# Latent items of a two-layer diffusion step: one multiplication per head, copies and squares ahead of the gate, three items' transposes behind the first scores

## The reference, cut to what matters

```python
aq, ak, av, bq_d, bkv_d, cq, ck, cv, gates = jnp.split(h @ p['w_in'], IN_SPLITS, axis=-1)
bq = (rms_norm(bq_d, p['mla_q_norm']) @ p['w_mla_q_up']).reshape(b, t, MLA_HEADS, MLA_QK_DIM)
bq = rms_norm(bq, p['mla_qk_norm'][0])
...
kv = (rms_norm(ckv, p['mla_kv_norm']) @ p['w_mla_kv_up']).reshape(b, s, MLA_HEADS, MLA_NOPE_DIM + MLA_V_DIM)
k = rms_norm(jnp.concatenate([k_nope, k_pe], axis=-1), p['mla_qk_norm'][1])
...
ck = rms_norm(ck.reshape(b, t, GQA_KV_HEADS, HEAD_DIM), p['gqa_qk_norm'][1])
```

## Time and profile before

| | us |
|---|---|
| median of 3 runs | 2578.64 (2576.64 to 2580.96) |
| the profiled execution | 2574.08 |
| its span | 2571.3 |
| PE busy in the span | 2485.4 (97%) |
| DVE busy | 1368.3 (53%) |
| ACT busy | 972.0 (38%) |
| POOL busy | 410.2 (16%) |
| mean granted clock of PE | 0.986 |

### The profile page before, as it was taken

One profiled execution on the slowest core, in us unless ns is written; L12 is line 12 of the kernel. 1 busy time (PEld: TensorE's weight loads), 2 busy tenths in 40 slices (PEclk: granted clock), 3 DMA queues, 4 the chain that ended last, 5 costly groups with the idle time before them and its releaser, 6 DMA issues.

```text
span 2571.3 us, 42771 instructions
## 1 busy us (share of the span) xinstructions
PE 2485.4 (97%) x17115; PEld 2262.6 (88%) x17115; DVE 1368.3 (53%) x2339; ACT 972.0 (38%) x1713; POOL 410.2 (16%) x362
## 2 busy tenths in 40 slices
PE   7999999999999999999999999999999999999998
PEld 5878977798799999999977799768978999999998
DVE  4675366736755454254446734765476545433542
ACT  5453255424534332133244523454254243322332
POOL 0500022022020221022014001220310202200220
PEclk8999999999999999999999999999999999999999
DMA  7312232422132222322322021322210412222222
GB/s 241 96 34 66 70 102 79 130 88 59 34 115 66 66 81 62 86 66 70 122 79 74 18 79 60 96 88 66 79 49 17 145 52 69 74 74 78 81 58 82
DMA packets 252834, 202.80 MB, mean 79 GB/s; under 512 B 9877, under 2 KB 235911, under 8 KB 252679
## 3 DMA queue, kind: packets, MB, share of 16 engines
q1 hardware_dynamic: 245574, 197.67, 25.5%
q10 hardware_dynamic: 7104, 2.95, 0.4%
HBM read 196.50 MB, written 4.10 MB: 78 GB/s over the span
## 4 chain that ended last, share of the span: by engine, by line
PE 89%; DVE 4%; ACT 4%; issue 1%; DMA 1%; SPq 1%; POOL 0%; ACTq 0%; POOLq 0%; DVEq 0%
PE ps L1376 48%; PE ps L1398 8%; PE ps L1549 6%; PE ps L1563 4%; PE ps L1590 4%; PE ps L1361 3%; PE ps L1363 3%; PE ps L1362 3%; PE ps L1488 1%; PE ps L1445 1%; PE ps L1251 1%; ACT prob L1834 1%; PE ps L1505 1%; PE ps L1508 1%; PE ps L1261 1%
## 5 line engine op out<-in xcount | busy, mean ns | idle before, releaser
L2056 DVE TENSOR_TENSOR wlo<-raw,whi 128x1024 fp32r<-128x1024 f32 (+4 forms) x284 | 357.4, 1259 | 431.7 <-ACT whi L1701 430.2
L1376 PE MATMUL ps<-hhi,whi 128*128 128x320 f32 x1856 | 425.7, 311 | 6.3 <-DVE wlo L2056 2.4
L1376 PE MATMUL ps<-hlo,whi 128*128 128x320 f32 x1856 | 424.1, 310 | 0.0
L1376 PE MATMUL ps<-hhi,wlo 128*128 128x320 f32 x1856 | 424.0, 310 | 0.0
L1701 ACT ACTIVATE whi<-raw 128x1024 fp32r<-128x1024 f32 (+4 forms) x284 | 277.6, 978 | 376.5 <-PE ps L1376 294.9
L1376 PEld LDWEIGHTS ps<-hhi,whi 128*128 128x128 f32 x1856 | 311.1, 188 | 8.7 <-DVE wlo L2056 3.8
L1376 PEld LDWEIGHTS ps<-hlo,whi 128*128 128x128 f32 x1856 | 311.5, 188 | 0.0
L1376 PEld LDWEIGHTS ps<-hhi,wlo 128*128 128x128 f32 x1856 | 311.4, 188 | 0.0
L2345 POOL TENSOR_TENSOR rstd<-smean,mhalf 128x4 f32<-128x4 f32 (+3 forms) x96 | 118.6, 1238 | 547.3 <-DVE smean L2106 546.5
L2130 DVE TENSOR_REDUCE negmax<-ps 128x1 f32<-128x640 f32 x192 | 151.1, 819 | 65.7 <-PE ps L1549 64.5
L1398 PE MATMUL ps<-hhi,whi 128*128 128x320 f32 x512 | 177.4, 346 | 0.5 <-issue 0.5
(11 more groups left out here) (248 smaller groups left out, 4344.4 us busy)
## 6 DMA issues: line engine op xcount, KB each, us to landing
raw<-in_w_up SPq DMA_DIRECT2D x88, 512.0 KB, 4.9
raw<-in_w_in SPq DMA_DIRECT2D x40, 1024.0 KB, 5.2
raw<-in_w_ada SPq DMA_DIRECT2D x29, 1024.0 KB, 5.1
raw<-in_w_down SPq DMA_DIRECT2D x16, 768.0 KB, 4.8
raw<-in_w_down SPq DMA_DIRECT2D x16, 640.0 KB, 4.5
adaw<-in_w_ada SPq DMA_DIRECT2D x8, 1024.0 KB, 11.2
raw<-in_w_o SPq DMA_DIRECT2D x8, 1024.0 KB, 5.2
raw<-in_w_branch_a SPq DMA_DIRECT2D x4, 1024.0 KB, 5.0
```

The source lines that it names most:

```text
L1376: mm = pe.matmul(out, w[:, sub, c], m[:, kt, o:o + HALF], start=first and i == 0 and a == 0, stop=last and i == len(ks) - 1 and a == 2)
L2056: dve.tensor_tensor(dst(wlo), src, dst(whi).bitcast(F32), ALU.subtract).then_inc(S["lo_ready"], 1)
```

## The change

1. Items with at most four heads in every group (`few_heads`: bq, the cached latent item, up and ck; aq, ak and cq have eight) are normalised by one SCALAR_TENSOR_TENSOR for each head: head times its `rstd` value times the gain. The semaphore between the two old multiplications goes.
2. In `finish` without late items (branch B only) the copies of items 3 and 4 and the squares of item 3 stand ahead of the whole gate; before, they stood behind it. The split of the weights after the gate's is asked for ahead of item 2's tick instead of inside `gate()`.
3. The transposes of the third last up item stand in `left`, behind the first scores, and no longer ahead of the `ada` step. The scores of cycle 1 wait for the copies of these transposes too.

```diff
@@ finish @@
-        accs(its[0:3], ())
-        for it in its[0:3]:
+        early = 3 if late else 5
+        accs(its[0:early], ())
+        for i, it in enumerate(its[0:3 if late else 4]):
+            if i == 2 and not late:
+                prefetch(2)
             add("tick", it=it)
         gate()
         for it in late:
             turn(it, 7)
-        accs(its[3:], ())
-        add("tick", it=its[3])
+        if late:
+            accs(its[3:], ())
+            add("tick", it=its[3])
         turn(its[0], 4)
@@ attention @@
-                add("score", turned=bool(left) and i == 2, **seq[i])
+                add("score", turned=bool(left) and i in (1, 2), **seq[i])
@@ mixers @@
             add("flush")
-            turn(its[-3], 4)
             ada()
...
-                      left=[lambda it=it: turn(it, 4) for it in its[-2:]])
+                      left=[lambda it=it: turn(it, 4) for it in its[-3:]])
@@ apply_norm of the vector engine, behind the wait for rstd @@
+                        if few_heads(it):
+                            for g, (c, nh, dh) in zip(it["gains"], it["groups"]):
+                                for h in range(nh):
+                                    x = st[:, c + h * dh:c + (h + 1) * dh]
+                                    ins = dve.scalar_tensor_tensor(out=x, in0=x, scalar=rstd[:, par, h0 + h:h0 + h + 1],
+                                                                   in1=gains[:, g:g + dh], op0=ALU.mult, op1=ALU.mult)
+                                h0 += nh
+                            ins.then_inc(S["gained" if it["rope"] else "item_ready"], 1)
...
+                            return
```

More of the change, by code:

```diff
@@ L76, with few_heads @@
 QUARTER, ADA_COST = 1.8, 1.4
+def few_heads(it):
+    return max(g[1] for g in it["groups"]) <= 4
 def prob_turns(s):
@@ L776, in signals @@
     if k == "tick":
-        out = dict(sqr_done=1, ss_ready=len(it["groups"]), ms_done=len(it["groups"]), rstd_ready=1, xh_ready=1)
+        out = dict(sqr_done=1, ss_ready=len(it["groups"]), ms_done=len(it["groups"]), rstd_ready=1, xh_ready=int(not few_heads(it)))
         if it["rope"]:
@@ L2079, in apply_norm @@
                         h0 = 0
+                        if few_heads(it):
[6 more added lines that the diff above has]
+                            ins.then_inc(S["gained" if it["rope"] else "item_ready"], 1)
+                            if it["rope"]:
+                                to_finish.append((it, at["gained"], at["cos_done"], at["sin_ready"]))
+                            return
                         for c, nh, dh in it["groups"]:
```

## The result

| | before | after |
|---|---|---|
| median, us (6 executions each) | 2577.64 (2574.28 to 2581.05) | 2561.47 (2560.10 to 2569.22) |
| ratio, 95% interval | | 0.9946 [0.9927, 0.9964] |
| profiled execution, its span | 2574.08, 2571.3 | 2560.1, 2558.3 |
| mean granted clock of PE in it | 0.986 | 0.99 |

The kernel is 0.54% faster.

The account below looks back on a forecast made before the run. PE was taken as the bound, busy 2485.4 of 2571.3 us. Gains of 2.9 (place A), 1.8 (place B) and 1.6 (clock) sum to 6.3 us, so 2578.64 becomes 2572.4 us, range 2566 to 2580.

Parts of the forecast that it names:

- the ceiling: Most the change could gain from PE's waits for copies of bq, copies of up and rotary sum: 11.7 us, 0.45%.
- Place A: Whole gate of branch B, twice: transposes follow the gate at once, the tanh is late next; 1.44 us each, -2.9 us.
- Place B: End of a half's up items, four times: PE's wait moves behind the scores, rotary sum ends it; 0.45 each, -1.8 us.
- 0.25 - 0.20 + 0.22 = 0.27: Place B: forecast terms were 0.25 us from last transposes ending earlier and 0.22 from two items' new multiplications.
- The size of the multiplications: On DVE: one head of 96 costs 319 ns, four overlapping 1.04 us, against 1.15 for the old pair.
- its 1.56 us: Low clock in layer 1's place A: 1.56 us lost in the profiled execution, counted as gone after the change.
- its 4.75: Low clock at place B, layer 1's second half: 4.75 us lost, counted as likely after the change as before.
- The 4.6 us between the median and the profiled execution: Profiled 2574.08 against median 2578.64, explained by more low-clock stretches in the other runs; distance kept in the forecast.
- R2: Rival: the clock gains more; both low stretches at the touched places go, giving 2567.6 us; chance 0.16.
- R1: Rival: the wait only moves; place B gives 0, place A 2.9 us, giving 2575.7, no change; chance 0.22.
- R3: Rival: slower; place B's moved wait makes low clock the rule in all four places, giving 2588 us; chance 0.09.
- R4: Rival: bq item 0 is late behind the copies, place A gives nothing; 2576.8 us, no change; chance 0.08.

Follow-up runs that it names:

- A filled: The kernel before, with 12 products that nobody reads put into PE's wait at both places A alone; measured 0.9974 [0.9955, 0.9993], 2569.89 us.

## Why the prediction was wrong

**Bounds: the ceiling was wrong.** "All its idle time is 86 us" counted only what PE waits. Before loses some 40 us to the clock on top, after 30: 40.1 of 2577.0 us is 1.6%, and 29.8 of 2563.9 is 1.2%. The Trainium skill, TensorE: Matmul & The Clock Gate, Part 1, puts the penalty of the warm-up at a kernel's start below 1% of a typical span and says that it varies from run to run. The traces agree for the start: from 10 to 45 us the mean clock was 0.80 in one trace of before and 0.71 in another, 7 and 10 us or 0.3 to 0.4%. The stretches later in the program come on top of that.

**Place A was right.** 1.38 and 1.40 us of 1.44, with the tanh as the next to be late, as worked out.

**Place B's position was right, its size too large.** The wait moved behind the scores and the rotary sum ends it. It gave 1.0 us in four places instead of 1.8: nothing in the first halves, and in the two second ones 0.4 and 0.6, near the forecast 0.45. The transposes behind a wait take 0.64 us and not 0.44, which takes back 0.2 of each place; that was my choice of the wrong row, since the earlier trace rows had 0.64 for the same four transposes. And DVE's stop of 0.26 us in the first halves takes back what the multiplications give. With 0.25 - 0.20 + 0.22 = 0.27 the second halves gave more than the terms; why stays open.

**The size of the multiplications was right**: 310 ns for 319, 1.00 us for 1.04. By the rule against small tiles that the prediction cites from the Trainium skill (VectorE: DVE Perf Modes, the trn2 errata) I had worked out 1.28 us for four without overlap. The trace does not bear that out: the four overlap (1.00 us for 4 x 0.31), while the two old instructions, with a semaphore between them, did not (1.15 us for 0.55 + 0.56).

**The step that failed is the clock**: "so I count its 1.56 us as gone ... I count its 4.75 as likely as before". 1.6 us were counted and about 10 measured (loss 40.1 to 29.8). Three things were wrong in it:
- The size was read from one execution. In that one, places A and B cost 6.0 us; over four it was 7.8, and the highest 10.9.
- The gap at B was taken to cost the clock after the change as before. But in the second halves the wait of 2.0 us became one of 1.5 behind the scores, in the first halves the waits of 0.8 and 1.1 us got an `ada` step and scores between them, and no low clock followed in any of 12 visits. That the length of one wait decides is a plausible reading (11 of 28 against 2 of 14 above); no run varied it alone, without its place.
- The 4.6 us between the median and the profiled execution were seen as low clock and then kept in the forecast. By the table of loss they were of the same kind as what the change removes; after the change the distance is 1.4 us.

Of the rivals, R2 named the cause (2567.6), and it too fell short, by 6 us, as its price was that of one execution. R1's picture is true of place B's first halves at full clock. R3 was wrong in sign: a shorter gap in the midst of short transposes didn't draw low clock. R4 did not occur.

**The sum now**: 2.8 (A) + 1.0 (B) + about 10 (clock) = 13.8, against 13.1 measured on the means. Of the 13.0 us between the spans of the profiled pair 3.8 are schedule, 6.0 clock at the touched places, and some 3 lie where no part of the change touches a wait, 1.6 of them by the low clock there (28.2 us before, 26.6 after).

## What to carry to other kernels

A wait of PE near 2 us between stretches of dense work has a second price, the slow stretch that sometimes follows it, and here that price (8 us over six places by the stretches' lengths, 10 to 12 by the mean loss) was higher than the waits' own length saved (3.8). Read it from several executions, as (1 - mean clock) x span, and not from one trace; and put unread products into the wait once, which tells what the clock is worth before any schedule is changed. Then prefer to fill such a wait with work that must be done anyway: a gate quarter moved to the right place gave 5.2 us more at full clock.

## What the runs showed of the hardware

- Which of equal waits is followed by low clock changes from execution to execution of the same kernel (10 of 24 visits, never the same set in four traces), while stretches at full clock repeat within 0.02 us.
- A low stretch at A cost 1.5 us and one at B 3.0 to 4.8 us.
- Low clock followed a wait of 1.9 to 2.0 us in 11 of 28 visits, two waits of 0.8 and 1.1 us with four transposes between in 2 of 14, and in none of 66 where the wait had been filled, shortened or moved.
- Four transposes of 96 columns take 0.44 us of PE's time in a running row and 0.64 behind a wait, mostly since they no longer overlap with the instruction ahead.
- In the kernels with the new multiplications DVE stood 0.26 to 0.28 us ahead of one rotary product, in both layers, with nothing in the profile to end it. What it is stays open.
- One execution of the kernel with A filled took 4487 us where the other eleven lay near 2570; its mean granted clock was 0.798. It is left out of the table, and no trace shows where it lost the time.
